# Expert layer of a two-block transformer: passes sorted by token count, four of them with 64 seats and two products, and down projections two units behind

## The reference, cut to what matters

```
def moe_swiglu(x, router_w, w_gate, w_up, w_down):
    logits = (x @ router_w).astype(jnp.float32)
    top_v, top_i = lax.top_k(logits, TOP_K)              # TOP_K = 2
    gates = jax.nn.softmax(top_v, axis=-1)
    combine = jnp.sum(jax.nn.one_hot(top_i, N_EXPERTS) * gates[..., None], axis=-2)
    y = jnp.zeros_like(x)
    for e in range(N_EXPERTS):                           # 8
        y = y + combine[..., e:e + 1] * swiglu(x, w_gate[e], w_up[e], w_down[e])
    return y
# swiglu(x) = (silu(x @ w_gate) * (x @ w_up)) @ w_down, with w_gate, w_up 1024 x 3584, w_down 3584 x 1024
```

## Time and profile before

| | us |
|---|---|
| median of 3 runs | 2625.47 (2623.07 to 2625.53) |
| span of the profiled execution, first to last instruction | 2620.8 |
| straight expert segment in it | 1595.3 to 2467.3 |
| TensorE / VectorE / ScalarE busy | 2532.1 / 1914.5 / 1399.9 |

### The profile page before, as it was taken

The page is one execution under the profiler, slowest core; times in us unless marked ns, Lnnn a source line. Parts: engine busy times, 40 slices in busy tenths (PEclk is TensorE's granted clock), DMA queues, the critical chain, the costliest instruction groups (busy, mean ns, idle before and its releaser), DMA issues.

```text
span 2620.8 us, 36271 instructions
## 1 busy us (share of the span) xinstructions
PE 2532.1 (97%) x14798; PEld 2195.6 (84%) x14798; DVE 1914.5 (73%) x2221; ACT 1399.9 (53%) x1490; POOL 0.2 (0%) x4
## 2 busy tenths in 40 slices
PE   7999999999999999999999999999999999999897
PEld 7999889899898998869988767888888888888786
DVE  7765755577675546956447958898989898988797
ACT  4554544456454433224333226777777777777674
POOL 0000000000000000000000000000000000000000
PEclk9999999999999999999999998999999999999999
DMA  6334545343345534215534117999999999999796
GB/s 252 131 128 145 201 185 193 136 155 136 114 176 199 187 150 175 97 37 221 193 145 147 49 58 270 358 362 351 355 359 358 353 352 356 354 355 361 286 355 259
DMA packets 119492, 593.19 MB, mean 226 GB/s; under 512 B 17440, under 2 KB 17824, under 8 KB 77216
## 3 DMA queue, kind: packets, MB, share of 16 engines
q1 hardware_dynamic: 110096, 585.40, 60.2%
q10 hardware_dynamic: 9232, 5.47, 0.8%
HBM read 589.79 MB, written 1.05 MB: 225 GB/s over the span
## 4 chain that ended last, share of the span: by engine, by line
PE 85%; DVE 12%; ACT 1%; issue 1%; DMA 1%; POOLq 0%; ACTq 0%; DVEq 0%
PE bank L2525 35%; PE bank L595 20%; PE bank L852 12%; PE bank L1704 3%; DVE big L2831 2%; PE bank L1120 2%; DVE ring_lo L826 2%; PE bank L2481 1%; PE bank L1135 1%; PE bank L1725 1%; PE bank L1890 1%; PE bank L2544 1%; DVE big L2112 1%; PE bank L1934 1%; DVE wlo L674 0%
## 5 line engine op out<-in xcount | busy, mean ns | idle before, releaser
L674 DVE TENSOR_TENSOR wlo<-ring,whi 128x2048 fp32r<-128x2048 f32 x430 | 981.4, 2290 | 167.1 <-ACT whi L669 161.7
L669 ACT ACTIVATE whi<-ring 128x2048 fp32r<-128x2048 f32 x433 | 827.9, 1914 | 132.3 <-PE bank L2525 109.7
L2525 PE MATMUL bank<-whi,xhi 128*128 128x512 f32 x896 | 362.3, 404 | 9.8 <-DVE wlo L674 7.8
L2525 PE MATMUL bank<-whi,xlo 128*128 128x512 f32 x896 | 352.3, 393 | 0.0
L2525 PE MATMUL bank<-wlo,xhi 128*128 128x512 f32 x896 | 350.7, 391 | 0.0
L826 DVE TENSOR_TENSOR ring_lo<-ring,slot_hi 128x1024 fp32r<-128x1024 f32 x160 | 192.4, 1222 | 130.1 <-ACT slot_hi L803 123.2
L595 PE MATMUL bank<-xhi,whi 128*128 128x256 f32 x864 | 245.8, 284 | 2.4 <-DVE xlo L557 1.3
L595 PE MATMUL bank<-xlo,whi 128*128 128x256 f32 x864 | 245.7, 284 | 0.0
L595 PE MATMUL bank<-xhi,wlo 128*128 128x256 f32 x864 | 245.6, 284 | 0.0
L803 ACT ACTIVATE slot_hi<-ring 128x1024 fp32r<-128x1024 f32 x160 | 166.6, 1053 | 106.8 <-PE bank L852 77.5
L852 PE MATMUL bank<-xh,slot_hi 128*128 128x256 f32 x704 | 202.4, 287 | 3.0 <-DVE ring_lo L826 3.0
(11 more groups left out here) (509 smaller groups left out, 4613.1 us busy)
## 6 DMA issues: line engine op xcount, KB each, us to landing
ring<-in_stream SPq DMA_DIRECT2D x555, 1024.0 KB, 6.6
par<-in_par ACTq DMA_DIRECT2D x2, 2048.0 KB, 9.3
con<-in_con SPq DMA_DIRECT2D x1, 1216.0 KB, 10.4
X<-in_x SPq DMA_DIRECT2D x2, 512.0 KB, 4.1
out_y<-X SPq DMA_DIRECT2D x2, 512.0 KB, 2.6
par<-in_par ACTq DMA_DIRECT2D x2, 448.0 KB, 5.9
par<-in_par ACTq DMA_DIRECT2D x2, 157.5 KB, 3.4
con<-in_con SPq DMA_DIRECT2D x1, 64.0 KB, 4.3
```

Source lines behind the costliest of these rows:

```text
L669: act.activation(whi[:, k % NSPLIT, :], src, ACT.Copy).then_inc(act_done, AC.step(tag + f".w{k}"))
L674: v.tensor_tensor(wlo[:, k % NSPLIT, :], src, whi[:, k % NSPLIT, :].bitcast(F32), ALU.subtract)\
L2525: mm = pe.matmul(out, left, right, start=start and i == 0, stop=stop and i == len(pairs) - 1)
```

## The change

**Sorted passes.** Pass 0 is still expert 0. The other seven are sorted on VectorE by count, smallest first (`v.max` on -8 x count + expert number); passes 1 to 4 are *narrow* (64 seats, `NARROW`), passes 0, 5, 6 and the loop's are *wide* (128 seats, `WIDE_PASS`). A pass's expert is now known only on the chip, so SyncE reads its number from `table` before the pass's first load and computes the addresses (`expert_of`, one table load for each of passes 1 to 6, and an address computation for most slots). An expert with more tokens than its pass has seats gets a further turn of the loop; up to four (`EXTRA`).

**Narrow passes.** The 64 tokens' high parts and low parts lie side by side in the 128 stationary columns of `xhi`. Each weight slot is then multiplied twice, by its high and by its low part: 16 matmuls for the ups and 8 for the down of a unit, in place of 24 and 12. The PSUM bank holds the high tokens' results in rows 0 to 63 and the low tokens' in rows 64 to 127. ScalarE copies the whole bank (128 x 512) to SBUF (`taken`), and four matmuls with a stacked identity (`fold`) turn it and add the two halves in one. SiLU, gate, high and low part follow on 128 columns, with SiLU and gate now behind the turn (`gate`, `gated`, `high`, `low`).

**Order.** `LAG` = 2: up0 g, up1 g, down g - 2. The last unit's turn is done ahead of the last two downs. The scatter, pick, put and gather steps of a pass move one unit later.

**The table.** The small instructions leave the place ahead of the first gather. `v_order_passes`, in three parts, runs in units 1, 2 and 3 of the first pass; the first pass's pick moves to unit 5, the scaling of X into Y to units 6 and 8. The low part of the segment's third slot moves behind the first pick.

On SyncE, a slot of passes 1 to 6 has one address instruction more than before for most slots, and nothing changes places. What stands on the other engines:

The diff, cut to its core:

```diff
-NPASS = NEXP + (2 * T) // (CAP + 1)
+NARROW = CAP // 2
+EXTRA = 4
+NPASS = NEXP + EXTRA
...
+LAG = 2
+WIDE_PASS = (0, 5, 6, 7)
...
-        if g:
-            order.append(("down", g - 1))
-    return order + [("down", units - 1)]
+        if g >= LAG:
+            order.append(("down", g - LAG))
+    return order + [("down", g) for g in range(units - LAG, units)]
...
+                    chosen = {0: 0}
+
+                    def expert_of(p):
+                        if p not in chosen:
+                            if len(chosen) == 1:
+                                sp.wait_ge(vec_done, VE.at("fe.table"))
+                            chosen[p] = sp.value_load(table[0:1, p:p + 1], min_val=0, max_val=NEXP - 1)
+                        return chosen[p]
...
-                            load_expert(sp, s, g // UNITS_EXP, kind, g % UNITS_EXP)
+                            load_expert(sp, s, expert_of(g // UNITS_EXP), kind, g % UNITS_EXP)
...
-                v_split_ahead(v, tag + "next", 2)
...
-                over, rank, hot, numf = small[:, 0:8], small[:, 8:16], small[:, 16:24], small[:, 60:60 + NPASS + 2]
...
-                for q in range(NPASS - NEXP):
-                    v.tensor_scalar(hot, rank, float(q + 1), None, ALU.is_equal).then_inc(vec_done, VE.step())
-                    v_wait(v)
-                    v.tensor_tensor(hot, hot, over, ALU.mult).then_inc(vec_done, VE.step())
...
+                v_split_ahead(v, tag + "next", 2)
+                v_gather(v, tag, 0, True)
...
+                high = xhi[:, block, at:at + n].bitcast(F32)
+                low = xlo[:, block, at:at + n] if wide else xhi[:, block, at + n:at + 2 * n]
...
-                    mm = products(out, ((xh, hi[:, j]), (xh, lo_[:, j]), (xl, hi[:, j])), first + j == 0,
-                                  first + j == KD - 1)
+                    pairs = [(xh, hi[:, j]), (xh, lo_[:, j])]
+                    if is_wide(g, rolled):
+                        pairs.append((xl, hi[:, j]))
+                    mm = products(out, pairs, first + j == 0, first + j == KD - 1)
...
             def turn(g):
+                if is_wide(g, rolled):
+                    pe.wait_ge(vec_done, VE.at(tag + f".h{g}"))
+                    for kk in range(2):
+                        mm = pe.transpose(PS[2 + g % 2][:, kk * CAP:(kk + 1) * CAP], hidc[g % 2][:, kk * P:(kk + 1) * P],
+                                          ident)
+                else:
+                    pe.wait_ge(act_done, AC.at(tag + f".b{g}"))
+                    pe.wait_ge(vec_done, VE.at(tag + ".fold"))
+                    for b in range(4):
+                        mm = pe.matmul(PS[2 + g % 2][:, b * NARROW:(b + 1) * NARROW],
+                                       both_halves[g % 2][:, b * P:(b + 1) * P], fold, start=True, stop=True)
                 mm.then_inc(pe_done, PE.step(tag + f".t{g}"))
...
-                            mm = products(PS[4 + f][:, :], ((hh_, hi[:, cols]), (hh_, lo_[:, cols]), (hl, hi[:, cols])),
-                                          u == 0 and kk == 0, u == UNITS_EXP - 1 and kk == 1)
+                            pairs = [(hh_, hi[:, cols]), (hh_, lo_[:, cols])]
+                            if is_wide(g, rolled):
+                                pairs.append((hl, hi[:, cols]))
+                            mm = products(PS[4 + f][:, :], pairs, u == 0 and kk == 0, u == UNITS_EXP - 1 and kk == 1)
...
+                if k == n - 3:
+                    turn(order[-1][1])
...
+            def taken(g):
+                if is_wide(g, rolled):
+                    if g >= 2:
+                        act.wait_ge(vec_done, VE.at(tag + f".h{g - 2}"))
+                    act.activation(silc[g % 2], PS[g % 2][:, 0:UNIT], ACT.Silu).then_inc(act_done, AC.step(tag + f".s{g}"))
+                else:
+                    if g >= 2 and not is_wide(g - 2, rolled):
+                        act.wait_ge(pe_done, PE.at(tag + f".t{g - 2}"))
+                    act.activation(both_halves[g % 2], PS[g % 2][:, :], ACT.Copy)\
+                       .then_inc(act_done, AC.step(tag + f".b{g}"))
...
+                    act.wait_ge(vec_done, VE.at(tag + f".h{g}"))
+                    to, src = hhi[:, g % 2, :, 0:NARROW], hidc[g % 2][:, 0:2 * NARROW]
...
+            def gate(g):
                 act.wait_ge(pe_done, PE.at(tag + f".t{g}"))
                 if g >= 2:
-                    act.wait_ge(pe_done, PE.at(tag + f".p{order.index(('down', g - 2))}"))
-                act.activation(hhi[:, g % 2, :, 0:CAP], PS[2 + g % 2][:, 0:2 * CAP].rearrange("p (k c) -> p k c", k=2),
-                               ACT.Copy).then_inc(act_done, AC.step(tag + f".hh{g}"))
+                    act.wait_ge(vec_done, VE.at(tag + f".h{g - 2}"))
+                act.activation(silc[g % 2][:, 0:2 * NARROW], PS[2 + g % 2][:, 0:2 * NARROW], ACT.Silu)\
+                   .then_inc(act_done, AC.step(tag + f".s{g}"))
...
+            def picked_sum(out, which, values, n):
+                v_wait(v)
+                y = terms[:, 0:n * NEXP].rearrange("p (r e) -> p r e", r=n)
+                v.tensor_tensor(y, which, rows_by(n, values), ALU.mult).then_inc(vec_done, VE.step())
+                v_wait(v)
+                v.tensor_reduce(out, y, AX.X, ALU.add).then_inc(vec_done, VE.step())
...
+                v.max(top[:, 1, :], top[:, 0, :]).then_inc(vec_done, VE.step())
+                v_wait(v)
+                v.max_index(topi[:, 0, :], top[:, 1, :], top[:, 0, :]).then_inc(vec_done, VE.step())
+                v_wait(v)
+                v.tensor_copy(num[:, 0:NEXP], topi[:, 0, :]).then_inc(vec_done, VE.step())
+                v_wait(v)
+                v.tensor_tensor(member_of, rows_by(NEXP, iota8), num[:, 0:NEXP].unsqueeze(2)
+                                .to_broadcast([P, NEXP, NEXP]), ALU.is_equal).then_inc(vec_done, VE.step())
+                for t in range(NT):
+                    picked_sum(place[:, t, 0:NEXP], member_of, at_expert[:, t, :], NEXP)
...
+            if part == 2:
+                picked_sum(num[:, NEXP:NPASS], spill, num[:, 0:NEXP], EXTRA)
+                v_wait(v)
+                v.tensor_copy(table[0:1, :], num[0:1, :]).then_inc(vec_done, VE.step(tag + ".table"))
...
+                if rolled is None and p == 0 and kind == "up1":
+                    if u == 0:
+                        v.tensor_tensor(fold, ident[:, 0:NARROW], ident[:, NARROW:2 * NARROW], ALU.add)\
+                         .then_inc(vec_done, VE.step(tag + ".fold"))
+                    if 1 <= u <= 3:
+                        v_order_passes(v, tag, u - 1)
...
```

More of the change, by code:

```diff
@@ L2517, in build, with is_wide @@
         hidc = [scr[:, 0, 512 + 256 * i:768 + 256 * i] for i in range(2)]
+        both_halves = [reset[:, i * 512:(i + 1) * 512] for i in range(2)]
+        fold = c("m8")[:, 0:NARROW]
+        at_expert = small[:, 80:80 + NT * NEXP].rearrange("p (t e) -> p t e", t=NT)
+        counts = small[:, 96:104]
+        num = small[:, 104:104 + NPASS + 2]
+        over_cap, rank, ones8, cap8 = (small[:, a:a + NEXP] for a in (120, 128, 136, 144))
+        member_of = small[:, 152:152 + NEXP * NEXP].rearrange("p (r e) -> p r e", r=NEXP)
+        spill = small[:, 216:216 + EXTRA * NEXP].rearrange("p (q r) -> p q r", q=EXTRA)
+        terms = small[:, 320:320 + NT * NEXP * NEXP]
+        def is_wide(g, rolled):
+            return rolled is not None or g // UNITS_EXP in WIDE_PASS
         def t_experts(pe, tag, order, rolled, ahead):
@@ L2596, in a_experts @@
             n = len(order)
+            last = order[-1][1]
             for k in range(LEAD):
@@ L2624, in a_experts @@
                 if kind == "up1" and g:
-                    turned(g - 1)
-                if k == n - 1:
-                    turned(g)
+                    after_turn(g - 1)
+                if k == n - 2:
+                    after_turn(last)
+                    if not is_wide(last, rolled):
+                        high(last)
                 if k + LEAD < n:
@@ L2662, in picks @@
                 for t in range(NT):
[L2663 removed]
+                    if rolled is not None or p + 1 in WIDE_PASS:
+                        out, seats = pick[:, t, :], c("iota")
+                    else:
+                        out = pick[:, t, :].rearrange("p (d c) -> p d c", d=2)
+                        seats = c("iota")[:, 0:NARROW].unsqueeze(1).to_broadcast([P, 2, NARROW])
+                    v.tensor_scalar(out, seats, to[:, t:t + 1], None, ALU.is_equal)\
                      .then_inc(vec_done, VE.step(at + ".pick" if t else None))
@@ L2692, in v_experts @@
                 if kind == "up1" and g:
-                    turned(g - 1)
-                if k == n - 1:
-                    turned(g)
+                    after_turn(g - 1)
+                if k == n - 2:
+                    after_turn(last)
+                    if not is_wide(last, rolled):
+                        low(last)
                 if k + LEAD < n:
```

220 lines of the change are left out of this document (126 added, 94 removed).

## The result

| us | before | after |
|---|---|---|
| median | 2624.39 (2623.07 to 2625.53, 4 runs) | 2550.75 (2547.49 to 2553.39, 4 runs) |
| profiled span | 2620.8 | 2545.5 |
| ratio of the times | | 0.9719 (0.9708 to 0.9731) |

The change takes 73.6 us off; forecast were 41, with 2556 as the lower end. The number of the rival in which loads come at 412 GB/s, 2553 us, is the nearest.

A forecast was written before the change was run, and what follows sets the result against it. TensorE was taken as the bound, VectorE 13% behind and DMA share near 1. Terms -42 (narrow passes), -2 (lag), -0.3 (sorting), +3 (table) gave -41.3: span 2579.5, median 2584 us, range 2556 to 2610.

The forecast's parts named there:

- the rival in which loads come at 412 GB/s: Narrow passes: VectorE binds if loads come at 412 GB/s or more; unit 7.6 us, -73, 2553 us; chance 0.13.
- the price of the loads: Narrow units: 3.146 MB a unit at 392 GB/s takes 8.03 us, 8.15 with meshing.
- the term for meshing: Narrow units: 0.12 us added because two near-equal bounds, VectorE 7.5 and loads 8.03, don't mesh.
- the term of -42: Four narrow passes: 56 units go from 8.90 to 8.15 us, -42 us, with ends -78 and -21.
- -2 and +3: -2 us: idle at two segment ends goes with the lag; +3 us: table's small instructions delay TensorE in the first pass.
- the turn on TensorE: Narrow units: four 64-column matmuls replace two transposes, taken as 0.26 us more than now.
- TensorE busy: Passes 1 to 4: stretches should show TensorE busy about 0.8, from 6.4 of 8.15 us a unit.
- "0" for the narrow chain: Narrow units: copy, fold, SiLU, gate, high, low fit with downs two units behind; cost 0, up to the 0.12 for meshing.
- VectorE as the bound of the whole narrow stretch: Narrow passes: VectorE binds if loads reach 412 GB/s or more; -73, 2553 us; chance 0.13.
- A lower DMA ceiling: Narrow passes: share 0.96 at 354 GB/s means a ceiling near 369; 8.53 us a unit, -21, 2605 us; chance 0.22.
- the cap at the present rate: Narrow passes: loads capped at 354 to 358 GB/s, 8.8 to 8.9 us a unit, 2620 us; chance 0.06.
- TensorE's clock: Narrow passes: clock falls to 1.2 GHz, +2.7 us a unit, +151 over 56 units, 2770 us; chance 0.05.

The follow-up runs named there:

- all passes wide: The changed kernel with all eight passes at 128 seats, sorting and the two-unit lag kept: 2623.88 us, ratio 0.9994 to the kernel before.
- half the bytes: The changed kernel with each slot's load in narrow passes bringing only half its columns, splits and products all done: 2542.65 us, ratio 0.9684.
- one unit behind: The changed kernel with `LAG` = 1 in place of 2, everything else as changed: 2767.63 us, ratio 1.0548 to the kernel before.
- table's work moved: The changed kernel with the table's three parts put behind the gate, in units 2 to 4 of the first pass: 2549.66 us, ratio 0.9714.

## Why the prediction was wrong

**The step that failed** is the price of the loads: "I take 392, the longest stretch above demand in the segment's own traffic, and 0.12 us for the two near-equal bounds (7.5 and 8.03) not meshing: 8.15 us." The unit is 7.60 us. The loads run at 413 GB/s, by which it would be 7.62, so of the term for meshing nothing shows. A pass of 107.3 us is 7.66 a unit with its scatter and gather, so the term of -42 should have been (8.90 - 7.66) x 56 = -69, and with a first narrow pass that begins with slots in store (3 us shorter than the others) the table shows -70.4. That is 28 of the 34 us by which the forecast missed the span (2579.5 against 2545.5). Of the rest, 3 are the start of the run, and 3 are that the other rows come to -1.8 together, where -2 and +3 were forecast. Against the kernel with all passes wide the narrow passes bring 73 us, some 3 more than in their rows, since cheaper matmuls of theirs fall into the rows of passes 0 and 5.

Why 392 was a bad choice: I read it as a ceiling, because it was the longest stretch above what I had worked out as demand. But at 2560 to 2580 us TensorE was busy 20.00 of 20; it waited for no load. Such a rate is no ceiling, whatever share the DMA engines show. The 412 at the segment's start and the 425 at the program's are, I think, of another kind: VectorE, which frees the slots, was busy only 7.15 and 6.32 of 10, at times when a segment fills its ring. That is a reading and not shown: in the first of them no engine waited for a load, in the second ScalarE waited 1.3 us for a slot. The narrow passes hold 413. The share of 0.96 at 354 GB/s says nothing on the ceiling: after the change it is 1.02 at 413, 6% more share for 17% more bytes.

**Right in the mechanism.** TensorE stops being the bound and the loads take its place; ScalarE's splits wait for slots to land. The four small experts fit 64 seats. The narrow steps of ScalarE and VectorE cost what the neighbouring rows said; the turn on TensorE cost 0.37 us more than forecast. VectorE's bound was put at 7.5; without scatter and gather it is 7.01, and with them (a pass of 104.9 us with half the bytes) 7.49.

**TensorE busy.** The forecast said about 0.8 of the narrow passes and the rows show 0.93 to 0.98. Its 6.4 us held the scatter and the gather (they are in the 8.90), but too cheap a turn, and its unit was too long; with 6.36 + 0.47 in 7.66 it would have been 0.89. A matmul's record is 0.39 us long where they start 0.227 apart, so each short stop is hidden in part by the record ahead of it.

**Lag.** "0" for the narrow chain is right with two units behind, and one unit behind shows what hung on it: 217 us. "Between units nothing waited for a down, so 0 in the wide units" is nearly right: 0.5 to 0.9 us a pass. The idle 1.02 us is gone from the end of the segment:

```profile
2385.95 0.38 PE L2530 MATMUL bank<-con,scr 128*128 128x128 f32 x2
2386.09 0.48 PE L2508 MATMUL bank<-whi,hhi 128*128 128x512 f32 x1
```

**The table.** +3 was forecast. The 48 small instructions take 8.4 us in the three units, not 9.6; TensorE stops for 1.99 and 0.53 us, where 2 to 3 were forecast, but the first stop comes in unit 1, whose downs the lag has taken away, so VectorE had less room than I counted. From the SiLU of unit 1 to that of unit 2 it takes 9.50 us, where the 24 matmuls and the turn need 5.7, and two units later 9.14 in place of 8.43: +4.5. Of the first 3.8 some 2.2 are the stop and 1.6 the lower clock behind it, a cost that the forecast didn't have. All of it goes into the zero that "all passes wide" shows in the sum.

**The rivals.** VectorE as the bound of the whole narrow stretch was right in its number (2553) and wrong in its mechanism: its condition, loads at 412 GB/s or more, held, but with VectorE's load cut in half nothing moved. Its own sum set 7.60 by the loads, and the name hid this. A lower DMA ceiling and the cap at the present rate are refuted by 413 GB/s over three passes. The Trainium skill (DMA: Bandwidth & Descriptors, "Where 436 GB/s comes from") says that the memory side binds loads from HBM at about 358; here one core drew 413. The Trainium skill (HBM Reference, "Specifications (TRN2)") says that a core streaming alone measures about 425. The 413 here is near that and far from 358, and I had not set the two pages against each other. TensorE's clock stayed at 0.98 or more in the change, but the rival was no fancy: one unit behind it fell to 0.81 to 0.86.

## What to carry to other kernels

A rate says where the ceiling is only if somebody waits for it: a stretch in which the consumer is full gives a lower bound and no more, however long it is. Here the 412 and 425 of two short stretches were nearer to the 413 measured later than the 392 of a longer one with TensorE full. When several engines are within a few per cent of one another, a busy share of 98% does not name the bound; halve one load at a time, and then both, and the step that appears only with both gives the order of the limits. Before two products are made out of three, count what the small steps between them take when each stands behind a long instruction in its engine's queue, and put the use of their result that far behind.

## What the runs showed of the hardware

- One core loads 1 MB slots at 411 to 413 GB/s for 315 us on end, beside TensorE, VectorE and ScalarE at 0.94, 0.98 and 0.87 busy.
- The DMA engines' share of busy time is no measure of what is left: 0.96 at 354 GB/s, 1.02 at 413, 0.64 at 212 and 0.73 at 234 with half of each slot's columns.
- Four matmuls of 64 columns with four different stationary blocks take 0.81 us, 0.2 each, as against 0.26 for two transposes of 128 columns. The gather's 16 matmuls of 128 columns take 0.22 each, so half the columns make next to nothing of a difference; what sets it no run here separates.
- One stop of 1.99 us (the change, first pass) was followed by some 3 us at TensorE's lower clock, which cost 1.6 us more. Stops of 1.08 and 1.36 us (table's work moved) were followed by none.
- With TensorE busy three quarters of the time in bursts with pauses of 2 to 4 us (one unit behind), the granted clock alternated between its levels and was 0.86 and 0.81 in two stretches of 100 us. In the narrow passes of the change, where TensorE waits 18 times for a weight's low part, 0.5 us in the mean, and three times some 2 us for the low part of an output, it was 0.98 to 1.00.
